# The last expert's results go to their tokens by a one-hot product; the norms' sums come as mean squares

## The reference

```python
def rms_norm_2(x, g, eps=EPS):
    xf = x.astype(F32)
    y = xf * lax.rsqrt(jnp.mean(xf * xf, axis=-1, keepdims=True) + eps)
    return (y * g.astype(F32)).astype(x.dtype)

def moe_swiglu(h, w_router, w_gate, w_up, w_down):
    logits = jnp.einsum('bsd,de->bse', h.astype(F32), w_router.astype(F32))
    top_val, top_idx = lax.top_k(logits, TOP_K_EXPERTS)
    top_w = jax.nn.softmax(top_val, axis=-1)
    combine = jnp.sum(jax.nn.one_hot(top_idx, N_EXPERTS, dtype=F32) * top_w[..., None], axis=-2)
    out = jnp.zeros_like(h)
    for e in range(N_EXPERTS):
        out = out + combine[..., e:e + 1].astype(h.dtype) * swiglu(h, w_gate[e], w_up[e], w_down[e])
    return out
...
        x = x + gt2 * f
    return rms_norm_2(x, g_final)
```

## Time and profile before

| | |
|---|---|
| Median of 3 runs | 2813.11 us (2810.33 to 2815.27) |
| The profiled execution, its own time | 2808.58 us |
| Its span in the trace | 2806.3 us |
| TensorE busy, share of the span | 2700.1 us, 96% |
| VectorE, ScalarE, GpSimd busy | 1075.6, 424.8, 175.4 us |
| Mean granted TensorE clock | 0.984 of full |
| Experts' products: first and last | 2062.78 us to 2781.20 us |
| From the last product to the end of the span | 25.1 us |

### The profile page before, as it was taken

One profiled execution on the slowest core, in us unless ns is written; L12 is line 12 of the kernel. 1 busy time (PEld: TensorE's weight loads), 2 busy tenths in 40 slices (PEclk: granted clock), 3 DMA queues, 4 the chain that ended last, 5 costly groups with the idle time before them and its releaser, 6 DMA issues.

```text
span 2806.3 us, 47103 instructions
## 1 busy us (share of the span) xinstructions
PE 2700.1 (96%) x20132; PEld 1790.3 (64%) x20132; DVE 1075.6 (38%) x2456; ACT 424.8 (15%) x1156; POOL 175.4 (6%) x285
## 2 busy tenths in 40 slices
PE   8999899999999998999999999999989999999996
PEld 7875457687778644577875658865546554556454
DVE  4772342367567504324774544444321001001011
ACT  1110252001101103220101321112311110111000
POOL 3100100000000002000000100001000000000001
PEclk9999999999999999999999999999999999999998
DMA  7954323366657542234764434544179999999996
GB/s 238 338 199 164 105 90 120 134 240 220 215 181 257 178 149 91 90 101 157 260 214 118 139 111 160 172 136 124 61 289 373 395 395 403 396 399 396 396 406 233
DMA packets 306002, 620.41 MB, mean 221 GB/s; under 512 B 15213, under 2 KB 172049, under 8 KB 305665
## 3 DMA queue, kind: packets, MB, share of 16 engines
q1 hardware_dynamic: 287088, 550.80, 54.6%
q0 software_dynamic: 18704, 66.56, 6.9%
HBM read 607.87 MB, written 9.44 MB: 220 GB/s over the span
## 4 chain that ended last, share of the span: by engine, by line
PE 85%; issue 8%; DVE 4%; DMA 1%; ACT 1%; POOL 1%; POOLq 0%; SPq 0%; DVEq 0%; ACTq 0%
PE psum L1108 20%; PE psum L1190 16%; PE psum L1067 12%; PE psum L1229 8%; PE psum L1582 5%; PE psum L1029 5%; PE psum L1320 3%; PE psum L1493 2%; PE psum L1603 2%; PE psum L1053 1%; PE psum L1056 1%; PE psum L1708 1%; PE psum L1660 1%; PE psum L1204 1%; DMA xn<-in_w_ada 1%
## 5 line engine op out<-in xcount | busy, mean ns | idle before, releaser
L1190 PE MATMUL psum<-ring,xT 128*32 128x512 f32 (+3 forms) x5376 | 464.5, 503 | 1.6 <-ACT xT L2012 1.6
L1067 PE MATMUL psum<-ring,hid 128*128 128x512 f32 x880 | 386.7, 592 | 0.0
L1190 PEld LDWEIGHTS psum<-ring,xT 128*32 128x32 f32 x5376 | 204.1, 110 | 247.0 <-issue 225.8
L1067 PEld LDWEIGHTS psum<-ring,hid 128*128 128x128 f32 x880 | 164.8, 190 | 195.6 <-issue 195.6
L2915 DVE SCALAR_TENSOR_TENSOR proj<-proj,psum 128x256 f32<-128x256 f32 (+1 forms) x72 | 28.5, 395 | 591.2 <-ACT proj L2026 591.2
L1229 PE MATMUL psum<-ring,proj 128*32 128x256 f32 x4224 | 233.1, 379 | 0.8 <-ACT proj L2038 0.8
L1229 PEld LDWEIGHTS psum<-ring,proj 128*32 128x32 f32 x4224 | 168.9, 110 | 66.6 <-issue 9.0
L1029 PE MATMUL psum<-ring,xT 128*128 128x512 f32 (+1 forms) x480 | 200.7, 580 | 2.1 <-DVE xT L2266 1.4
L1108 PE MATMUL psum<-xT,ring 128*128 128x128 f32 x1600 | 195.0, 275 | 0.0
L1108 PEld LDWEIGHTS psum<-xT,ring 128*128 128x128 f32 x1600 | 187.1, 192 | 0.3
L1029 PEld LDWEIGHTS psum<-ring,xT 128*128 128x128 f32 x480 | 91.2, 191 | 109.8 <-issue 107.3
(11 more groups left out here) (422 smaller groups left out, 3130.9 us busy)
## 6 DMA issues: line engine op xcount, KB each, us to landing
ring<-in_ffn_w_gu SPq DMA_DIRECT2D x88, 1024.0 KB, 6.6
ring<-in_w_exp_down SPq DMA_DIRECT2D x88, 1024.0 KB, 8.9
ring<-in_w_exp_gate SPq DMA_DIRECT2D x128, 512.0 KB, 7.0
ring<-in_w_exp_up SPq DMA_DIRECT2D x128, 512.0 KB, 9.0
ring<-in_ffn_w_down SPq DMA_DIRECT2D x44, 1024.0 KB, 9.8
xn<-in_w_ada POOLq DMA_DIRECT2D x24, 1024.0 KB, 8.8
proj<-in_w_ada POOLq DMA_DIRECT2D x24, 1024.0 KB, 9.0
ring<-in_w_exp_gate SPq DMA_DIRECT2D x64, 384.0 KB, 5.6
```

The costliest lines, as they stand in the source:

```text
L1067: ins = mm(banks[2 * b + h][:, :], hid[f][:, b * P:(b + 1) * P], rows[:, f, h * 512:(h + 1) * 512], start=first, stop=last, skip_group_che ...
L1190: ins = mm(o[:, :, o0:o1], xg[e % 2][:, k, 32 * g:32 * g + 32], w_[:, :, c0:c1], start=(k == 0 and n_ == 0), stop=(k == KT - 1), skip_grou ...
```

## The change

1. **The last expert's results.** The results of expert 7 no longer go to DRAM. A new `select(7)` on VectorE builds its one-hot matrix `sel` during expert 0. `turn_last`, between units 2 and 3 and between units 6 and 7 of `gate_up(7, 0)`, turns it on TensorE in eight products with the identity (two of 96 columns, six of 32 columns whose output lies on the partitions 96 to 127), and ScalarE copies it out in four instructions. After the last `down`, `scatter_last` multiplies it with `ye`: two products of 128x512 over 96 rows; then, for each block of tokens, one of 256 columns over 96 rows and three of 256 columns over the 32 rows 96 to 127. VectorE adds the four pieces of 128x512 to `x`, weighted by `comb`. `result` signals after each of its two instructions.
2. **The other experts' rows.** The four indirect DMAs wait only for the results of experts 0 to 6 and stand in GpSimd's queue behind the write of expert 6. A token's place at expert 7 points to the row of zeros (`RESULTS`). VectorE's four additions (`take`) stand between `hidden(7, 1)` and `hidden(7, 2)`.
3. **The branch.** VectorE reads the largest number of tokens early, ahead of `places`; its branch stands behind the four additions of the last products.
4. **Norms.** ScalarE squares x/32, so that the sums are mean squares; `mean_squares` is one instruction. `final` becomes an ordinary norm with four pieces of 512 columns and one root for both blocks.

The core of the diff (constants of the semaphores' counts and of the late branch left out):

```diff
 SLOTS = NEXP * CAP
+RESULTS = SLOTS - CAP
+ROOT_MEAN = 1 / 32
...
+        selT_last = [qT[CAP:P, 0, :], qT[CAP:P, 1, :], kTt[CAP:P, 0, :]]
...
+                        if e == NEXP - 1:
+                            break
 
                         t, to = ye[e % 2], result_rows[e * CAP:(e + 1) * CAP, :]
-                        pool.wait_ge(sm["ye_dve"], e + 1)
+                        pool.wait_ge(sm["ye_dve"], 2 * e + 2)
...
-                        pool.wait_ge(sm[f"results_out{i}"], 16 * NEXP)
+                        pool.wait_ge(sm[f"results_out{i}"], 2 * 16 * ((NEXP - i) // 2))
...
+                def turn_last(part):
+
+                    pe.wait_ge(sm["chosen_ready"], 4)
+                    pe.wait_ge(sm["gath_evac"], 2 * NEXP + part)
+                    for b in range(NB):
+                        if part == 0:
+                            mm(banks[7][0:CAP, b * P:(b + 1) * P], sel[:, b, 0:CAP], ident, start=True, stop=True, skip_group_check=True)
+                        for g in ((0, 1), (2,))[part]:
+                            at = S * (g % 2) + b * P
+                            ins = mm(banks[7][CAP:P, at:at + P], sel[:, b, 32 * g:32 * g + 32], ident, start=True, stop=True,
+                                     skip_group_check=True)
+                    ins.then_inc(sm["gath_psum"], 1)
+
+                def scatter_last():
+                    t = ye[(NEXP - 1) % 2]
+                    pe.wait_ge(sm["gath_evac"], 2 * NEXP + 2)
+                    pe.wait_ge(sm["ye_dve"], 2 * NEXP - 1)
+                    for b in range(NB):
+                        mm(banks[b][:, :], selT[0:CAP, b * P:(b + 1) * P], t[0:CAP, 0:512], start=True, stop=True)\
+                            .then_inc(sm["scat_ready"], 1)
+                    pe.wait_ge(sm["ye_dve"], 2 * NEXP)
+                    for b in range(NB):
+                        bank = banks[(2, 7)[b]]
+                        mm(bank[:, 0:256], selT[0:CAP, b * P:(b + 1) * P], t[0:CAP, 512:768], start=True, stop=True, skip_group_check=True)
+                        for g in range(GROUPS):
+                            ins = mm(bank[:, 256:512], selT_last[g][:, b * P:(b + 1) * P], t[CAP:P, 256 * g:256 * g + 256],
+                                     start=False, stop=(g == GROUPS - 1), skip_group_check=True)
+                        ins.then_inc(sm["scat_ready"], 1)
...
-                    gate_up(e, 0, lambda k: None)
+                    gate_up(e, 0, lambda k: turn_last(k // 4) if e == NEXP - 1 and k in (2, 6) else None)
...
                 down(NEXP - 1, 2)
+                scatter_last()
...
-                        A_(xn[:, b, cut], x[:, b, cut], ACT.Square, accum_out=ssq[:, 2 * h + b:2 * h + b + 1])\
+                        A_(xn[:, b, cut], x[:, b, cut], ACT.Square, scale=ROOT_MEAN, accum_out=ssq[:, 2 * h + b:2 * h + b + 1])\
...
+                        if e == NEXP - 1:
+                            act.wait_ge(sm["gath_psum"], 2 * NEXP + 1)
+                            A_(selT[0:CAP, :], banks[7][0:CAP, 0:S], ACT.Copy)
+                            for i in range(2):
+                                ins = A_(selT_last[i], banks[7][CAP:P, i * S:(i + 1) * S], ACT.Copy)
+                            ins.then_inc(sm["gath_evac"], 1)
+                            act.wait_ge(sm["gath_psum"], 2 * NEXP + 2)
+                            A_(selT_last[2], banks[7][CAP:P, 0:S], ACT.Copy).then_inc(sm["gath_evac"], 1)
...
-                link(V.tensor_tensor(mean[:, :], ssq[:, 0:2], ssq[:, 2:4], ALU.add))
-                V.tensor_scalar(mean[:, :], mean[:, :], 1.0 / D, EPS, ALU.mult, ALU.add).then_inc(sm["mean_sq"], 1)
+                V.scalar_tensor_tensor(mean[:, :], ssq[:, 0:2], EPS, ssq[:, 2:4], ALU.add, ALU.add).then_inc(sm["mean_sq"], 1)
...
-                    for b in range(NB):
-                        dve.wait_ge(sm["norm_ssq"], 4 * n0["norm"] + 2 * b + 2)
-                        V.tensor_scalar(mean[:, b:b + 1], ssq[:, b:b + 1], 1.0 / D, EPS, ALU.mult, ALU.add).then_inc(sm["mean_sq"], 1)
+                    mean_squares(st)
+                    dve.wait_ge(sm["rsqrt_done"], n0["roots"] + 1)
...
-                        link(V.tensor_scalar(place_sum[:, 1, :], place_sum[:, 0, :], float(SLOTS), None, ALU.min))
+                        link(V.tensor_scalar(place_sum[:, 1, :], place_sum[:, 0, :], float(RESULTS), None, ALU.min))
...
+                    def take():
+
+                        for b in range(NB):
+                            dve.wait_ge(sm[("rows_in", "last_rows_in")[b]], (16 * (NEXP + 1), 32)[b])
+                            for m in range(2):
+                                link(V.scalar_tensor_tensor(x[:, b, :], taken[b][m], stat[:, 28 + 2 * m + b:29 + 2 * m + b], x[:, b, :],
+                                                            ALU.mult, ALU.add))
+
+                    select(0)
                     shares()
+                    most_now = dve.value_load(most_i[0:1, 0:1], min_val=0, max_val=S)
                     places()
...
                             result(e - 1)
+                        else:
+
+                            dve.wait_ge(sm["gath_psum"], 2)
+                            select(NEXP - 1)
                         hidden(e, 1)
+                        if e == NEXP - 1:
+                            take()
                         hidden(e, 2)
                     result(NEXP - 1)
+                    for i, (b, h) in enumerate(pieces("h")):
+                        dve.wait_ge(sm["scat_ready"], i + 1)
+                        xs = x[:, b, h * 512:(h + 1) * 512]
+                        V.scalar_tensor_tensor(xs, banks[(0, 1, 2, 7)[i]][:, :], comb[:, b, NEXP - 1:NEXP], xs, ALU.mult, ALU.add)\
+                            .then_inc(sm["x_part"], 1)
...
-                    with dve.If(dve.value_load(most_i[0:1, 0:1], min_val=0, max_val=S) > CAP):
+                    with dve.If(most_now > CAP):
...
-                    for b in range(NB):
-                        dve.wait_ge(sm[("rows_in", "last_rows_in")[b]], (16 * (NEXP + 1), 32)[b])
-                        for m in range(2):
-                            ins = V.scalar_tensor_tensor(x[:, b, :], taken[b][m], stat[:, 28 + 2 * m + b:29 + 2 * m + b], x[:, b, :],
-                                                         ALU.mult, ALU.add)
```

More of the change, by code:

```diff
@@ L890, in _ @@
                     hybrid(st)
-                if st["kind"] == "final":
-                    for b in range(NB):
-                        pool.wait_ge(sm["mean_sq"], n0["roots"] + b + 1)
-                        nc.gpsimd.tensor_tensor(rs_col[:, st["rs"], b:b + 1], mean[:, b:b + 1], minus_half[:, 0:1], ALU.pow)\
-                            .then_inc(sm["rsqrt_done"], 1)
-                if st["kind"] == "norm":
+                if st["kind"] in ("norm", "final"):
                     pool.wait_ge(sm["mean_sq"], n0["roots"] + 1)
@@ L1906, in _ @@
                     hybrid(st)
[L1907 to L1912 removed]
+                if kind in ("norm", "final"):
                     if n0["norm"]:
```

40 lines of the change are left out of this document (15 added, 25 removed).

## The result

| | before | after |
|---|---|---|
| Median of the runs (5 and 5) | 2813.11 us (2810.33 to 2815.27) | 2797.73 us (2794.99 to 2798.50) |
| Ratio, 95% interval | | 0.9944 [0.9931, 0.9956] |
| The profiled execution, its span | 2808.58, 2806.3 us | 2798.50, 2796.6 us |

The change makes the kernel faster by 15.8 us [12.4, 19.4] by the ratio, 15.4 us by the medians.

What follows compares the result with a forecast made beforehand. TensorE was taken to set the pace until 2781 us, followed by a 25.1 us tail. Terms -10.4 + 2.0 - 1.4 = -9.8 us gave 2798.8 us profiled, plus 4.5 us for the median: 2803.3 us, range 2800 to 2808.5.

Steps and rivals of the forecast that it cites:

- Part 1: Tail after the last product: falls from 25.1 to 14.7 us, -10.4 us.
- Part 2: TensorE in expert 7: `turn_last` adds eight products, 16 instructions, +2.0 us, range 1.7 to 2.8.
- Part 3: Moved gathers beside expert 7's weights: cost them 5.2 us of landing against 5.8 us to spare; charged nothing.
- Part 4: Seven early norms: one small instruction and its link go, 0.2 us each on the path, -1.4 us.
- the forecast's own sum: Whole span: -10.4 + 2.0 - 1.4 = -9.8 us.
- The branch: Rival: VectorE's taken branch between last addition and mean is exposed by 1.4 us, 2804.7 us; 12%.
- The weights: Rival: gathers exceed the spare time in expert 7, TensorE stalls 0.5 to 5.2 us, up to 2808.5; 10%.
- the gathers not starved: Denied rival: weights served first, gathered rows land at 2779.5, TensorE waits 13.0 us, 2816.3 us; 3%.
- The scatter at half clock: Rival: clock falls at once after the last `down`, the scatter's 5.2 us double, 2808.5 us; 4%.

Runs made afterwards that it cites:

- Experiment 11: The changed kernel with unused products in early norms and routing, `turn_last` as six transposes instead of eight products: 2787.01 us, ratio 0.9900 to the kernel before.
- experiment 10: The changed kernel with the four gathers doubled, into tiles nobody reads any more: 2803.17 us, ratio 0.9956 to the kernel before.
- the fills: Unused products of constants on TensorE in the seven early norms' rests, added to the kernel before: 2798.14 us (0.9948), and 2802.32 us (0.9962) on another chip.
- the filled kernels: Kernels with unused products in the early norms; adding the short mean to the kernel before so filled: 2798.14 to 2797.85 us, and 2802.32 to 2799.98 us.
- experiments 1 to 4: Ratios to the kernel before: that kernel again 0.9998, changed kernel again 0.9954, kernel before with short mean in 12 norms 0.9981, changed kernel with longer mean 0.9970.
- 6: The kernel before with unused products of constants on TensorE in the seven early norms: 2798.14 us, ratio 0.9948.
- 15: The kernel before with unused products in the seven early norms, repeated on another chip: 2802.32 us, ratio 0.9962.
- chip A: The chip of the first follow-up group; the changed kernel, unchanged, against the kernel before there: 2800.66 us against 2812.54, ratio 0.9954.

## Why the prediction fell short

**Part 1, the tail, -10.4: right, 0.7 us too much.** The trace has -9.7. All 0.7 us are in the scatter. The eight narrow products took 4.49 us (2783.82 to 2788.31) where 3.46 + 0.16 were streaming and latency; 0.3 of the rest is the clock at the very end, and 0.6 stands at the changes between products over 96 and over 32 rows. There are three such changes, not four, and each costs 0.20 us: the two instructions of 2783.82 take 0.52 us until the next starts, the six from 2784.34 take 1.49 and the two from 2785.83 0.63, where streaming gives 0.43, 1.30 and 0.43. The forecast took 0.3 for all of them. The Trainium skill, "TensorEngine Tiling (Array Packing)", section Key Properties, says that a change of the tiling mode drains TensorE. These rows agree. VectorE's addition cost 0.75 us, not 0.69. The root took 0.72 us, as a root without VectorE beside it.

**Part 2, `turn_last`, +2.0: measured +2.3**, inside 1.7 to 2.8. Experiment 11 shows that six transposes do it for 1.0.

**Part 3, the gathers, nothing: right.** They went out at 2720.77 to 2724.61, landed 8 to 12 us later, and the additions (2735.54 to 2740.78) waited for nothing. The load of `down(7, 0)` landed 3.2 us later than before and was still early. In experiment 10, with twice the gathers, TensorE still does not wait for the ring, so the cover is larger than the 5.8 us that the forecast counted; the 2.3 us that it loses there have another cause, which stays open.

**Part 4, the norms, -1.4: this is the step that failed.** The wait went down by exactly 1.4 us, but the short mean is worth 5.3 us [2.8, 7.9] alone and 4.3 (means) on top of the experts' part. The prediction had the rows of an early norm, the wait for the diagonal and the granted clock of 0.984 before it, and priced the clock only where the change was large, in the scatter. It did not ask what the 0.016 of clock that were missing belonged to. In the profiled execution of before they are 44.0 us of full clock: 6.8 at the early norms, 6.8 at the routing, 9.9 in the tail, where it costs nothing, and 20.5 elsewhere. That the norm's part can be had is shown by the fills, worth 14.6 and 10.7 us. That the short mean's surplus is clock is supported by both accounts (4.3 of 4.9 us, 4.3 of 4.3; 9.4 us lost at the norms instead of 15.4), but not shown: in the filled kernels, where the norms are quiet, it is worth 0.6 and 4.2 us by the ratios, and both the path's 1.4 and the unfilled 5.3 are possible there. With experiments 1 to 4 in it the forecast's own sum would read -8.2 - 5.3 = -13.5, 2799.6 us, and the time measured is 2797.7.

**The pair of traces.** That its difference, 9.7 us, is the forecast's 9.8 is an accident. In it the stretch before the experts brought 2.35 us, and before's profiled execution was one that lost little at the norms. A single execution of this kernel lies anywhere in 11.7 us.

**The rivals.** The branch was not exposed (0.03 us). The weights were not late and the gathers not starved. The scatter at half clock came true only at its very end, where it cost 0.3 us.

**What stays open.** The excess does not grow with the dose: 3.9 us for one instruction, 10.1 for five whose path is 7, 2.7 in the filled kernel with two more products. A window of 20 us around one norm reads 1.00, 0.91 or 0.83, and which norms fall differs between executions of one kernel; how many fall for a given rest was not found. What makes the clock fall at the places outside norms and routing, the largest part of the loss, was not studied. The fills don't silence the clock fully either: the same kernel, 6 and 15, read 0.9886 and 0.9864 on two chips, 4 us apart. Nor is the difference between the first measurement (-15.8) and chip A (-12.9) explained; the intervals overlap.

## What to carry to other kernels

Where the granted clock is below 1.00 in the mean, find the places where it falls before pricing an edit near them: edits of 0.2 us beside such rests were measured at some three times their path or more (one interval reaches down to the path), and products that nobody needs, put into the rests, were worth nearly as much as this whole change (14.6 and 10.7 us; together with it 25 to 28 us). A result that goes through DRAM at the very end of a kernel can go by a product instead, if that path costs less than write, fetch and add; here 9.7 us were won with 2.3 us of TensorE's time. And one profiled execution gives the terms of a sum well, but not its level: compare it with the spread of the runs before matching a difference of a few us to it. Last, a stall beside extra transfers is not yet a late transfer: see in the list of waits whether the engine waited for one.

## What was not expected of the hardware

- Two rests of 1.70 and 1.13 us in a norm that TensorE goes through at 2.4 GHz are enough for the clock to fall behind it (0.72 in the 6 us after), in some executions and not in others; with rests of 0.84 and 0.26 us it stayed at 1.00.
- Executions of one kernel on one chip differ by 11.7 us (2806.9 to 2818.6, 22 runs), and the mean granted clock, 0.980 to 0.984, orders them roughly.
- A write of 96 KB under the full stream of weights landed in 5.9 us, and gathers of 512 KB in 7.8 to 11.8 us, while the DMA engines went on moving 403 GB/s in all: the two queues shared them, and that of GpSimd was not starved. Eight gathers instead of four left the weights in time, and TensorE still lost 2.3 us beside them.
- A change between float32 products over 96 rows and over 32 rows cost 0.20 us each time, three times in the scatter.
